# Value pages issued from GpSimd, the first pair's sample queries spread before the own-key mask, and a weight tile loaded between key pages

## The reference

```python
k_past = cache_k[l][page_table].reshape(Bs, past_len, N_HEADS, HEAD_DIM)
v_past = cache_v[l][page_table].reshape(Bs, past_len, N_HEADS, HEAD_DIM)
proj = rmsnorm(x, g_mix_pre) @ w_in          # q, k, v, conv input, gelu input, gates
logits = q @ k.T * HEAD_DIM ** -0.5 + rel_bias[t5_bucket(rel)]
logits = where(mask, logits, -1e30)
o_attn = softmax(logits) @ v
o_rnn = rglru(conv(xr)) * gelu(gb)
x = x + rmsnorm((sigmoid(gate_a) * (o_attn @ w_pa) + sigmoid(gate_r) * (o_rnn @ w_pr)) @ w_out)
x = x + rmsnorm((silu(f @ w_gate) * (f @ w_up)) @ w_down)
```

## Time and profile before

| | |
|---|---|
| median of 3 runs | 780.96 us (779.69 to 781.68) |
| the profiled execution, its own time | 781.89 us |
| span of the profiled execution | 779.8 us |
| busy in the span: PE, DVE, ACT, POOL | 766.1, 482.4, 357.2, 70.4 us |
| instructions | 16411 |
| moved by DMA | 91.68 MB, 118 GB/s on average |

### The profile page before, as it was taken

How to read it: one execution, slowest core, us unless ns; L and a number is a source line. 1 busy time by engine, 2 the same in 40 slices (tenths; PEclk the granted TensorE clock), 3 DMA queues, 4 the chain that set the end, 5 groups by cost and what they waited for, 6 DMA issues and landing times.

```text
span 779.8 us, 16411 instructions
## 1 busy us (share of the span) xinstructions
PE 766.1 (98%) x5975; PEld 724.2 (93%) x5975; DVE 482.4 (62%) x756; ACT 357.2 (46%) x625; POOL 70.4 (9%) x156
## 2 busy tenths in 40 slices
PE   8999999999999999999999999999999999999996
PEld 6879999999899899997799999999999999999996
DVE  4655756847647634774567987887777777222323
ACT  5436534534625532334456555455555565222322
POOL 5521102102012010004000000000000010000000
PEclk9999999999999999999999999999999999999998
DMA  6745655555544224516552333233333125434333
GB/s 191 180 110 114 161 127 111 151 131 123 142 110 111 65 85 142 183 55 182 169 163 55 109 108 99 83 87 108 108 108 107 55 76 169 117 94 107 90 92 126
DMA packets 196979, 91.68 MB, mean 118 GB/s; under 512 B 65142, under 2 KB 190538, under 8 KB 196940
## 3 DMA queue, kind: packets, MB, share of 16 engines
q1 hardware_dynamic: 194270, 84.63, 40.0%
q0 software_dynamic: 2576, 6.45, 2.7%
q10 hardware_dynamic: 94, 0.09, 0.1%
HBM read 82.37 MB, written 6.81 MB: 114 GB/s over the span
## 4 chain that ended last, share of the span: by engine, by line
PE 94%; POOL 2%; DMA 1%; ACT 1%; issue 0%; DVE 0%; DVEq 0%; POOLq 0%; ACTq 0%
PE ps L958 32%; PE ps L1312 27%; PE ps L1377 17%; PE ps L1211 6%; PE ps L1281 3%; PE ps L1070 1%; PE ps L1084 1%; PE ps L1102 1%; PE ps L987 1%; DMA bias_rev<-dist_shift 1%; PE ps L1144 1%; PE ps L1055 1%; PE ps L1219 1%; PE ps L1115 1%; PE ps L990 0%
## 5 line engine op out<-in xcount | busy, mean ns | idle before, releaser
L1923 DVE TENSOR_TENSOR w_lo<-w_raw,w_hi 128x1024 fp32r<-128x1024 f32 (+1 forms) x67 | 80.1, 1197 | 131.7 <-ACT w_hi L1450 131.4
L958 PE MATMUL ps<-xin_hi,w_hi 128*128 128x272 f32 x576 | 125.4, 297 | 2.1 <-DVE w_lo L1923 1.0
L1450 ACT ACTIVATE w_hi<-w_raw 128x1024 fp32r<-128x1024 f32 (+1 forms) x68 | 70.0, 1030 | 119.3 <-PE ps L1377 78.1
L958 PE MATMUL ps<-xin_hi,w_lo 128*128 128x272 f32 x576 | 120.4, 288 | 0.0
L958 PE MATMUL ps<-xin_lo,w_hi 128*128 128x272 f32 x576 | 120.2, 288 | 0.0
L958 PEld LDWEIGHTS ps<-xin_hi,w_hi 128*128 128x128 f32 x576 | 90.4, 189 | 10.9 <-issue 7.6
L958 PEld LDWEIGHTS ps<-xin_lo,w_hi 128*128 128x128 f32 x576 | 91.1, 189 | 0.0
L958 PEld LDWEIGHTS ps<-xin_hi,w_lo 128*128 128x128 f32 x576 | 90.6, 189 | 0.0
L1377 PE MATMUL ps<-hid_hi,w_hi 128*128 128x272 f32 (+2 forms) x352 | 75.4, 289 | 0.4 <-DVE hid_lo L2339 0.4
L1377 PE MATMUL ps<-hid_lo,w_hi 128*128 128x272 f32 (+2 forms) x352 | 74.9, 288 | 0.0
L1377 PE MATMUL ps<-hid_hi,w_lo 128*128 128x272 f32 (+2 forms) x352 | 74.9, 288 | 0.0
(11 more groups left out here) (337 smaller groups left out, 1748.8 us busy)
## 6 DMA issues: line engine op xcount, KB each, us to landing
w_raw<-in_w_in_dram SPq DMA_DIRECT2D x72, 256.0 KB, 3.5
g_raw<-in_w_gate_up_dram SPq DMA_DIRECT2D x40, 256.0 KB, 3.7
w_raw<-in_w_down_dram SPq DMA_DIRECT2D x40, 256.0 KB, 3.0
u_raw<-in_w_gate_up_dram SPq DMA_DIRECT2D x20, 256.0 KB, 3.1
e_raw<-in_w_gate_up_dram SPq DMA_DIRECT2D x20, 256.0 KB, 4.2
kc<-in_cache_k_dram SPq DMA_DIRECT2D x64, 64.0 KB
vc<-in_cache_v_dram SPq DMA_DIRECT2D x64, 64.0 KB
wo_raw<-in_w_out_dram SPq DMA_DIRECT2D x12, 256.0 KB, 4.1
```

The costliest lines, as they stand in the source:

```text
L958: mm = e.matmul(ps[:, bank + h, 0:HT], wt[:, kw, :], xt[:, kx, h * HT:h * HT + HT], start=first and wt is wh and xt is xh, stop=last and ( ...
L1450: e.activation((to or w_hi[s])[:, 0:k, :], w_raw[s][:, 0:k, :], ACT.Copy).then_inc(hi_done, count)
L1923: e.tensor_tensor(wl[:, 0:k, :], w_raw[s][:, 0:k, :], wh[:, 0:k, :].bitcast(F32), ALU.subtract).then_inc(lo_done, count)
```

## The change

1. GpSimd reads the 16 page numbers into registers of its own, six after it has issued dist_bias and ten after the four bias_rev transfers, both places where it then waits for data.
2. GpSimd issues all value pages. In pair 0 they follow the pair's four copies, in one run of 16; for pair it + 1 they follow the gelu polynomial of pair it and wait for `mi_ready`. SyncE issues none.
3. In pair 0 the spread of the sample queries comes right behind the bias copies, then the own-key mask, then the four copies. In other pairs the order stays.
4. SyncE loads tile 2 after six key pages instead of after all sixteen, and pair 1's key pages now follow the table of the other pairs: four each at j = 4, 5 and 6, two at 7 and two in the next pair. KC_PAGES_0 goes.

```diff
-KC_PAGES_0 = (), (), (), (), (), range(0, 4), range(4, 9), range(9, 14)
...
-                    if j in (2, 4) and first:
-                        load_values(0, range(4 * j - 8, 4 * j))
-                    if j < 4 and not first:
-                        if j == 0:
-                            load_keys(it, KC_REST)
-                            e.wait_ge(mi_ready, it * 5 - 3)
-                        load_values(it, range(4 * j, 4 * j + 4))
-                        if j == 3:
-                            e.wait_ge(mi_free, it * 5 - 3)
-                            store_kv(it - 1)
+                    if j == 0 and not first:
+                        load_keys(it, KC_REST)
+                    if j == 3 and not first:
+                        e.wait_ge(mi_free, it * 5 - 3)
+                        store_kv(it - 1)
...
-                    pages = (KC_PAGES_0 if first else KC_PAGES)[j]
+                    pages = KC_PAGES[j]
...
-            load_keys_0()
+            load_keys_0(range(6))
             load(2, 0, wi[:, :, 2 * 512:2 * 512 + P])
+            load_keys_0(range(6, DEC_B * NPG))
             load(3, 1, wi[:, :, 3 * 512:3 * 512 + P])
...
+            e.wait_ge(page_in, 16)
+
+            def page_numbers(js):
+                return [e.value_load(pages[0:1, j:j + 1], min_val=0, max_val=n_phys - 1) for j in js]
+
+            page = page_numbers(range(6))
             e.wait_ge(bias_moved, 16 * DEC_T + 16)
...
+            page += page_numbers(range(6, DEC_B * NPG))
             e.wait_ge(bias_moved, 16 * (DEC_T + 1 + PAIRS))
...
+            def load_values(it):
+
+                for j in range(DEC_B * NPG):
+                    src = cache_v[0].rearrange("n t h d -> n t (h d)")[bass.ds(page[j], 1), :, bass.ds(it * P, P)]
+                    e.dma_start(vc[:, j, :], src.rearrange("o (i a) c -> a (o i) c", i=BLK)).then_inc(vc_in, 16)
...
+            def pair(it, first=False, last=False):
+
+                if first:
+                    e.wait_ge(consts, C_ZERO + PAIRS + DEC_B)
+                    spread(it)
+                    e.wait_ge(q_spread, 1)
+                    own_mask()
+                    ready(it)
+                    load_values(it)
+                else:
+                    ready(it)
+                    e.wait_ge(it_ready, it + 1)
+                    spread(it)
...
+                if not last:
+                    e.wait_ge(mi_ready, it * 5 + 2)
+                    load_values(it + 1)
...
+            pair(0, first=True)
+            with e.Fori(1, PAIRS - 1) as it:
+                pair(it)
+            pair(PAIRS - 1, last=True)
```

More of the change, by code:

```diff
@@ L606, in load_keys, with load_keys_0 @@
                                 ).then_inc(kc_in, 16)
-            def load_keys_0():
-                for j in range(DEC_B * NPG):
+            def load_keys_0(pages):
+                for j in pages:
                     e.dma_start(kc[:, j, :], page_of(cache_k, 0, j).rearrange("o t c -> t (o c)")).then_inc(kc_in, 16)
[L613 to L617, removed]
             def store_blocks(out, buf, it):
@@ L847, in _, with own_mask, ready @@
                               ).then_inc(consts, 1)
-            for f in range(PAIRS):
-                own = bias_s[:, f, PAST:KS].rearrange("p (j g t) -> p j g t", j=NJ, g=NG)
-                e.wait_ge(consts, C_ZERO + PAIRS + DEC_B + 2 * f)
-                e.affine_select(out=own, in_=own, compare_op=ALU.is_ge, fill=NEG,
-                                base=0, pattern=[[-8, NJ], [-GR, NG], [0, DEC_T]], channel_multiplier=1).then_inc(consts, 1)
-                e.wait_ge(consts, C_ZERO + PAIRS + 1 + DEC_B + 2 * f)
-                e.affine_select(out=own, in_=own, compare_op=ALU.is_ge, fill=NEG,
-                                base=7, pattern=[[8, NJ], [GR, NG], [0, DEC_T]], channel_multiplier=-1).then_inc(consts, 1)
-            with e.Fori(0, PAIRS) as it:
+            def own_mask():
+                for f in range(PAIRS):
+                    own = bias_s[:, f, PAST:KS].rearrange("p (j g t) -> p j g t", j=NJ, g=NG)
+                    e.wait_ge(consts, C_ZERO + PAIRS + DEC_B + 2 * f)
+                    e.affine_select(out=own, in_=own, compare_op=ALU.is_ge, fill=NEG,
+                                    base=0, pattern=[[-8, NJ], [-GR, NG], [0, DEC_T]], channel_multiplier=1).then_inc(consts, 1)
+                    e.wait_ge(consts, C_ZERO + PAIRS + 1 + DEC_B + 2 * f)
+                    e.affine_select(out=own, in_=own, compare_op=ALU.is_ge, fill=NEG,
+                                    base=7, pattern=[[8, NJ], [GR, NG], [0, DEC_T]], channel_multiplier=-1).then_inc(consts, 1)
+            def load_values(it):
+                for j in range(DEC_B * NPG):
+                    src = cache_v[0].rearrange("n t h d -> n t (h d)")[bass.ds(page[j], 1), :, bass.ds(it * P, P)]
+                    e.dma_start(vc[:, j, :], src.rearrange("o (i a) c -> a (o i) c", i=BLK)).then_inc(vc_in, 16)
+            def ready(it):
                 count = e.to_reg(it + 1)
@@ L868, in _, with spread @@
                               ).then_inc(it_ready, 1)
+            def spread(it):
                 count = e.to_reg(it * 4 + 2)
@@ L872, in _ @@
                 e.wait_ge(tile_free[0], count)
-                e.wait_ge(it_ready, it + 1)
                 for h in range(2):
```

## The result

The changed kernel takes 786.29 us (median of 8 runs, 784.62 to 789.86); the kernel before, beside it, 780.17 us (8 runs, 777.23 to 784.2). The ratio is 1.0091, 95% interval 1.0075 to 1.0108: **slower by 0.9%, some 6 to 7 us**, where 779.2 and no measurable change were forecast, in a range of 778.0 to 782.0. The profiled execution took 786.54 us.

What follows compares the result with a forecast made beforehand. TensorE, busy 766.1 of 779.8 us, bounds the kernel. The terms sum to -1.74 us, all from the wait for the spread, the rest zero or covered: 779.2 us on the median of 780.96, range 778.0 to 782.0.

Steps and rivals of the forecast that it cites:

- Pairs 1 to 3 ... Pages are in some 40 us before their use. Zero.: Sixteen value page issues per pair move behind gelu on GpSimd, from 68.1 to about 78 us; effect zero.
- Keys of pair 1 one place earlier ... Zero: SyncE issues four key pages, then tile 5 at 47.9 us, usable at about 55.8, wanted after 58.3; effect zero.
- The rival of slow landings: Transfers take 5.7 us to land, so TensorE waits 0.3 us for keys and 1.1 for values: 780.6 us; chance 0.12.
- The rival in which VectorE's multiplies hold up GpSimd's issues: VectorE's SBUF multiplies make pair 0's value pages 1.7 us later: up to 780.3 us; within values late, chance 0.15.
- The 1.74 us: TensorE's idle time before pair 0's sample scores, waiting for GpSimd's spread, goes when the spread precedes the mask: -1.74 us.
- GpSimd's loads: Sixteen page number loads on GpSimd at 0.57 us each with gaps make the bias copies start 0.66 us late.
- Value pages: Pair 0's value pages on GpSimd issue every 0.60 us from about 45.0 to 54.0 us; nothing on the path.
- The spread: In pair 0, GpSimd's spread of the sample queries ahead of the mask is done at 39.22 us.
- The own values: TensorE begins pair 0's sample values at 58.30 us without a wait, the pages in at 56.7 to 57.7.
- Tile 2 behind six key pages: The last key page leaves SyncE at 27.1 us, in at 29.2 to 30.2, before TensorE's key turn; nothing gained or lost.

Runs made afterwards that it cites:

- e6: The changed kernel with GpSimd's value pages of pairs 1 to 3 waiting until ScalarE has made the high part of the next pair's tile 0: 780.14 us, 1.0006.
- e4: The changed kernel with the value pages of pairs 1 to 3 back on SyncE in their old places: 780.11 us, 1.0013.
- e11: The kernel before with only the new table for pair 1's keys, all values on SyncE: 786.12 us, 1.0083.
- e2: The changed kernel with the old table for pair 1's keys in pair 0, value pages still on GpSimd: 786.35 us, 1.0086.
- e13: The kernel before, unchanged, run again for a third trace; wait for the spread 0 us, no median given.
- e8: The kernel before with the spread ahead of the mask and weight tile 2 behind six key pages: 779.24 us, 0.9997.
- e9: The changed kernel with the later value pages of pairs 1 to 3 and the old table for pair 1's keys: 780.91 us, 1.0023.
- e3: The changed kernel with the old table for pair 1's keys and pair 0's value pages back on SyncE: 787.38 us, 1.0098.
- e12: The changed kernel with the values of pairs 1 to 3 on SyncE and the old table for pair 1's keys: 779.74 us, 1.0008.
- e15: The kernel before, unchanged, run again for a fourth trace; wait for the spread 1.12 us, no median given.
- e7: The changed kernel with key pages of pairs 1 to 3 moved as 128 pieces of 512 bytes, for timing only: 779.97 us, 1.0018.
- e10: The changed kernel with the values of pairs 1 to 3 issued by SyncE at the time GpSimd issued them: 800.04 us, 1.0263.

## Why the prediction was wrong

**The step that failed: "Pairs 1 to 3 ... Pages are in some 40 us before their use. Zero."** I compared the pages with their own use and never with what SyncE issues at that time. The burst began at 70.14 (68.1 forecast) with tile 0 of pair 1 and four key pages still to go; ScalarE got that tile at 86.65 instead of 81.33 us. The term came out at some 6 us instead of zero: e6, in which only this burst starts later, is within 1.5 us of the kernel before where the changed kernel is 6 to 7 slower, and e4, in which the burst is not there, is 0.75 above it (0.1 to 2.0 by its interval). So it is this collision, and not the queue by itself. The trace of before gave the warning, in a row that I did not take: ScalarE idled 2.18 us for tile 0 of pair 1 there, until 81.33.

**"Keys of pair 1 one place earlier ... Zero" failed too, for less.** It had the issue right (47.9 forecast, 48.25 found) and asked when TensorE begins tile 5. It should have asked what stands behind that tile on the engines that split it: in program order VectorE makes tile 5's low part before it adds the bias for the next turn, so the cover ended at 57.53 - 2.44 = 55.1 us, not at 58.3. With 3.7 us to land the tile would have been in at 53.6, in time; the issue of 3.50 instead of 2 us and the landing of 6.3 took it, and TensorE lost 2.44 us in this trace. e11 shows that the place of the keys can stall alone, e2 that the old place removes this stall. Its net price is small: e4 still has it (1.35 us), and the wait for the keys (1.33), and is only 0.75 us above before.

The rival of slow landings named the circumstance (keys and values beside each other in the DMA engines) but priced it only for the transfers it had in view, at 780.6 us, not for the weight tile between them, and had no term for issues that take longer. The rival in which VectorE's multiplies hold up GpSimd's issues did not come: the 64 issues of value pages took 675 to 737 ns, two multiplies of 512 columns (at 48.97 and 49.67 us) among them.

**What held.** The 1.74 us did go in the profiled run, though the forecast took a wait of one trace for a wait of every run (e13 has none). GpSimd's loads: 290 ns, about 0.50 us each with gaps against 0.57. But they did set the bias copies: the last load starts at 29.9 us and the copies at 30.56. The copies begin 5.04 to 5.32 us after the bias issues end in all nine traces with page loads, and 3.09 to 3.79 us after in six of the seven later traces without them (4.36 in e8). That delay of some 1.5 us was hidden from me by the first trace, whose rows took 5.14 us to come. Value pages: 0.675 us each against 0.60. The spread: done by 36.8 us (39.2 forecast). The own values at 57.85, forecast 58.3, no wait.

**Tile 2 behind six key pages** was booked at nothing and the keys at 29.2 to 30.2 us. The last key page was issued at 27.85, and TensorE, waiting for it, began at 31.73, 3.9 us later. Early in this run, it had waited 1.63 us; in e8 it waited 0.63, in e9 and in the traces with the late start (e3, e6, e12) not at all. It buys nothing (tile 2's low part is waited for as before), and by e8's median it costs nothing that can be told.

The Trainium skill, DMA: Bandwidth & Descriptors, "Issuing engines are not separate DMA queues", says that issuing from several engines at once saves sequencer time only, since all run on the same 16 DMA engines and interleave. The runs agree, in that the move freed SyncE's issue time and no more of it shows, and they add a price: SyncE's issues themselves became slower, 2.99 us a key page at the median of five in e3 against 0.97 in the same place in e15. The section "Queues, rings and completion order" of the same page of the Trainium skill has each DMA engine alternate between queues packet by packet. That could slow the key pages' small packets beside the value pages' larger ones, but no run here isolates it.

## What to carry to other kernels

Before moving transfers to another engine's queue, list what the first engine still issues in that stretch, and ask which in-order engine consumes the first late one and what it has queued behind it. A burst belongs behind the transfer that is needed next; a single wait placed there was worth 6 us here. And read a wait in several traces before booking its removal: the one that this change was good for came out at 1.74, 1.14, 1.12 and 0 us.

## What the hardware showed that I had not expected

- GpSimd's issue of value pages pauses after every 31 pages, whatever their split over pairs: 5.80 and 6.39 us in the changed kernel (after 16 + 15, and again after 1 + 16 + 14 pages), 5.56 in e6, 6.03 in e9, 7.14 in e3 (pair 0 not on GpSimd, so in pair 2); the second pause of e6 and e9 was shorter, 3.98 and 3.84. It costs nothing where GpSimd idles anyway; in e9 a wait of 1.62 us followed. What it waits for was not tried.
- An issue on SyncE is not a fixed price: a key page of 512 pieces of 128 bytes took 1.01 us at the median in the four traces of the kernel before, where GpSimd moves no pages, but from 0.57 to 3.40. With GpSimd's pages in flight it took up to 4.24 in the changed kernel (in 80.7 to 86.5) and 6.53 in e2, and the first issue of the weight tile behind it up to 4.16.
- Idle TensorE can be paid twice, and the length of the idle time alone doesn't say when. Waits of 2.02 (e7), 2.38 (changed kernel) and 2.45 us (e10) brought 3.4 to 3.5 us at 1.2 GHz, waits of 4.51 (e2) and 5.45 us (e11) 6.8 us; in e2 and e11 the first 0.9 us of that lay still inside the wait. But waits of 1.63, 1.74 and 2.44 us (before 61.77 in the changed kernel) left the clock at 2.4 GHz. The twin of the last, the same turn in e10, did not:

```profile
61.02 0.90 PE L1118 MATMUL ps<-ident,lgt 128*128 128x128 f32 x3 [2.45 <-DVE lgt L2076]
```
